# Seven-product pairs in a two-layer decoder trunk: partial sums seeded into the PSUM banks instead of added behind them

## What is computed

```python
for layer in range(2):                 # D = 2048, 256 tokens, fp32
    if layer == 0: h = h + fox_mixer(rmsnorm(h, g), ...)        # 16 heads of attention
    else:          h = h + retention_mixer(rmsnorm(h, g), ...)  # 8 heads, q/k 256, v/gate 512 wide
    h = h + square(relu(rmsnorm(h, g) @ w_up)) @ w_down         # D_FF = 8192
return rmsnorm(h, final_norm)
```

## Time and profile before

| | us |
|---|---|
| median of three executions | 2486.71 |
| span of the profiled execution, first to last instruction | 2485.3 |
| TensorE busy | 2474.5 |
| VectorE busy | 1915.0 |
| ScalarE busy | 1402.3 |
| mean granted TensorE clock | 0.999 |

### The profile page before, as it was taken

One profiled execution on the slowest core, in us unless ns is written; L12 is line 12 of the kernel. 1 busy time (PEld: TensorE's weight loads), 2 busy tenths in 40 slices (PEclk: granted clock), 3 DMA queues, 4 the chain that ended last, 5 costly groups with the idle time before them and its releaser, 6 DMA issues.

```text
span 2485.3 us, 30031 instructions
## 1 busy us (share of the span) xinstructions
PE 2474.5 (100%) x11128; PEld 2050.7 (83%) x11128; DVE 1915.0 (77%) x2118; ACT 1402.3 (56%) x1689; POOL 158.6 (6%) x272
## 2 busy tenths in 40 slices
PE   9999999999999999999999999999999999999998
PEld 7888888888888888888888888888888888888887
DVE  6455555887978888987778868778988888788787
ACT  7454445554646555655556545656565555464564
POOL 0000000100100000101110001000010000010010
PEclk9999999999999999999999999999999999999999
DMA  8445456675756766766665665666677666666584
GB/s 312 158 155 182 140 200 218 214 253 182 260 202 222 248 208 229 237 212 204 219 225 184 231 201 183 199 206 233 236 248 245 207 231 229 211 237 237 192 273 146
DMA packets 148503, 534.83 MB, mean 215 GB/s; under 512 B 18704, under 2 KB 18960, under 8 KB 147472
## 3 DMA queue, kind: packets, MB, share of 16 engines
q1 hardware_dynamic: 131040, 476.65, 55.1%
q0 software_dynamic: 17184, 56.11, 7.9%
q10 hardware_dynamic: 144, 0.26, 0.0%
HBM read 506.74 MB, written 26.21 MB: 214 GB/s over the span
## 4 chain that ended last, share of the span: by engine, by line
PE 53%; DVE 2%; issue 1%; DMA 1%; ACT 1%; POOL 0%; DVEq 0%; ACTq 0%; POOLq 0%
PE acc L905 9%; PE acc L907 9%; PE acc L906 9%; PE sc L907 7%; PE sc L906 7%; PE sc L905 7%; PE mix L906 1%; PE mix L907 1%; PE mix L905 1%; DVE w_lo L1916 1%; ACT w_hi L1339 0%; DMA raw<-in_w_stream 0%; DMA evac<-park 0%; PE tr L1054 0%; PE tr L703 0%
## 5 line engine op out<-in xcount | busy, mean ns | idle before, releaser
L1916 DVE TENSOR_TENSOR w_lo<-raw,w_hi 128x1024 fp32r<-128x1024 f32 x696 | 847.1, 1230 | 290.4 <-ACT w_hi L1339 287.8
L1339 ACT ACTIVATE w_hi<-raw 128x1024 fp32r<-128x1024 f32 x696 | 727.8, 1058 | 571.8 <-PE sc L907 185.3
L905 PE MATMUL acc<-w_hi,xT_hi 128*128 128x512 f32 x826 | 322.6, 391 | 1.0 <-DVE xT_lo L1981 0.6
L907 PE MATMUL acc<-w_hi,xT_lo 128*128 128x512 f32 x826 | 321.6, 389 | 0.0
L906 PE MATMUL acc<-w_lo,xT_hi 128*128 128x512 f32 x826 | 321.5, 389 | 0.0
L1339 ACT ACTIVATE w_hi<-scratch 128x1024 fp32r<-128x1024 f32 x201 | 211.8, 1057 | 169.3 <-PE acc L907 74.4
L1916 DVE TENSOR_TENSOR w_lo<-scratch,w_hi 128x1024 fp32r<-128x1024 f32 x201 | 244.7, 1220 | 68.1 <-ACT w_hi L1339 67.5
L905 PE MATMUL sc<-w_hi,xT_hi 128*128 128x512 f32 x736 | 287.4, 390 | 0.0
L907 PE MATMUL sc<-w_hi,xT_lo 128*128 128x512 f32 x736 | 286.6, 389 | 0.0
L906 PE MATMUL sc<-w_lo,xT_hi 128*128 128x512 f32 x736 | 286.4, 389 | 0.0
L905 PE MATMUL acc<-w_hi,aT_hi 128*128 128x512 f32 x600 | 233.8, 390 | 0.0
(11 more groups left out here) (279 smaller groups left out, 3930.5 us busy)
## 6 DMA issues: line engine op xcount, KB each, us to landing
raw<-in_w_stream SPq DMA_DIRECT2D x725, 512.0 KB, 4.6
scratch<-in_w_stream SPq DMA_DIRECT2D x171, 512.0 KB, 4.8
park<-stage POOLq DMA_DIRECT2D x38, 512.0 KB, 3.2
evac<-park POOLq DMA_DIRECT2D x152, 128.0 KB, 3.2
gain<-in_gains POOLq DMA_DIRECT2D x4, 1024.0 KB, 8.1
qk_park<-evac POOLq DMA_DIRECT2D x8, 512.0 KB, 4.8
scratch<-qk_park POOLq DMA_DIRECT2D x32, 128.0 KB, 5.3
h<-in_x SPq DMA_DIRECT2D x2, 1024.0 KB, 8.7
```

The lines of the kernel that those rows point to most:

```text
L905: pe.matmul(bank[:, :], x_hi, w_hi[:, c], start=start, stop=False, skip_group_check=True)
L907: return pe.matmul(bank[:, :], x_lo, w_hi[:, c], start=False, stop=stop, skip_group_check=True)
L1339: act.activation(w_hi[:, slot * SW:(slot + 1) * SW], mlp_raw(u, load_of(u, t)), ACT.Copy).then_inc(mlp_hi, 1)
L1916: dve.tensor_tensor(w_lo[:, c], mlp_raw(u, load_of(u, t)), w_hi[:, c].bitcast(F32), ALU.subtract).then_inc(mlp_lo, 1)
```

## The change

Three partial sums are written into PSUM banks ahead of the products that use them, and these products accumulate onto them. With P1 in bank x after B11 and P5 in `mix[1]` after TAU1:

- `seed_u` (ScalarE): x is copied to `mix[0]`; TAU2 accumulates there and gives U.
- `copy_p5` (ScalarE): `mix[1]` is copied to SBUF.
- `seed_z` (ScalarE): U is copied from `mix[0]` to z; TAU3 accumulates there and gives V in z.
- `seed_e` (VectorE): e = P5 - U; B22 accumulates.
- `seed_w` (VectorE): w = P5 - z, which must be read between TAU3 and TAU4; the products of block 1, token tile 1 accumulate.

The lead-in's order becomes B11, TAU1, TAU2, B21, TAU3, B22, TAU4. Each output is complete in its bank: `copy_t1`, `copy_p7`, `u_part`, `v_part`, `g_part`, `fold` and `sum_to` are gone. Signs of S2 and S4 change in the sums. VectorE's `tau13` is split: `tau3` comes after `lo(B21)`. In `value_gate_pair` both seeds of VectorE come after `lo(TAU4)` and both `rotated` after the seeds; in `seven_pair` `seed_w` comes before `lo(7)` and the second `turn_blocks` after it. Gates of six heads are read by `silu` from the bank; heads 3 and 7 get a copy (`gate_copy`).

```diff
-B11, TAU1, TAU3, B21, TAU2, B22, TAU4 = range(SEVEN)
+B11, TAU1, TAU2, B21, TAU3, B22, TAU4 = range(SEVEN)
...
@@ gpsimd, head
-                    pool.wait_ge(silu_made[t], hd + 1)
+                    if ends_half(hd):
+                        pool.wait_ge(silu_made[t], hd // RET_HALF + 1)
+                    else:
+                        pool.wait_ge((e_out, w_out)[t], UNITS[head_unit(hd) + 1].pairs + 1)
...
@@ tensor, seven_pair
                 pe.wait_ge(s_lo, unit.sums)
-                wait(pe, v_made, unit.sevens)
+                wait(pe, p5_out, unit.sevens)
                 wait(pe, o_out, TOKS * heads_done)
                 block_sum(u, TAU1, mix[1], lambda kk: s_part(up, S1, kk), True, True)
-                pe.wait_ge(w_out if after_block else z_out, unit.pairs)
-                block_sum(u, TAU3, z, lambda kk: s_part(up, S3, kk), True, True)
-                pe.wait_ge(t1_out, unit.sevens + 1)
+                pe.wait_ge(u_seeded, unit.sevens + 1)
+                block_sum(u, TAU2, mix[0], lambda kk: s_part(up, S2, kk), False, True)
                 block_sum(u, B21, x, lambda kk: x_part(lhs, 0, 2 + kk), False, False)
                 between(B21)
-                wait(pe, u_made, unit.sevens)
-                block_sum(u, TAU2, mix[0], lambda kk: s_part(up, S2, kk), True, True)
...
-                block_sum(u, B22, e, lambda kk: s_part(up, S4, kk), True, False)
+                pe.wait_ge(z_seeded, unit.sevens + 1)
+                block_sum(u, TAU3, z, lambda kk: s_part(up, S3, kk), False, True)
+                between(TAU3)
+                pe.wait_ge(e_seeded, unit.sevens + 1)
+                block_sum(u, B22, e, lambda kk: s_part(up, S4, kk), False, False)
                 between(B22)
-                pe.wait_ge(p7_out, unit.sevens + 1)
+                pe.wait_ge(w_seeded, unit.sevens + 1)
                 block_sum(u, TAU4, z, lambda kk: x_part(lhs, 1, 2 + kk), False, False)
...
@@ scalar
+            def seed_u(u, heads_done=0):
+                wait_used(act, u, B11)
+                wait(act, e_seeded, UNITS[u].sevens)
+                wait(act, o_out, TOKS * heads_done)
+                act.activation(mix[0][:, :], banks_of(u)[0][:, :], ACT.Copy).then_inc(u_seeded, 1)
+            def copy_p5(u, parts=mlp_parts):
+                wait_used(act, u, TAU1)
+                wait(act, w_seeded, UNITS[u].sevens)
+                act.activation(parts[1], mix[1][:, :], ACT.Copy).then_inc(p5_out, 1)
+            def seed_z(u, after_block=False):
+                wait_used(act, u, TAU2)
+                act.wait_ge(w_out if after_block else z_out, UNITS[u].pairs)
+                act.activation(banks_of(u)[1][:, :], mix[0][:, :], ACT.Copy).then_inc(z_seeded, 1)
...
@@ scalar, value_gate_pair
-                hi(u, TAU2)
+                hi(u, TAU3)
                 hi(u, B22)
+                seed_u(u, hd)
                 for t in range(TOKS):
                     act.wait_ge(qk_done[t], hd + 1)
                     act.activation(evac[t][:, :], banks_of(u - 1)[t][:, :], ACT.Copy,
                                    scale=factor(t, rstd)).then_inc(qk_out[t], 1)
-                copy_t1(u, sums_made, ret_parts)
                 hi(u, TAU4)
-                copy_p7(u, ret_parts)
+                copy_p5(u, ret_parts)
+                seed_z(u, after_block=True)
...
@@ vector
+            def seed_e(u, parts=mlp_parts, after_block=False):
+                dve.wait_ge(p5_out, unit.sevens + 1)
+                dve.wait_ge(z_seeded, unit.sevens + 1)
...
+                dve.tensor_tensor(banks_of(u)[2][:, :], parts[1], mix[0][:, :], ALU.subtract).then_inc(e_seeded, 1)
+            def seed_w(u, parts=mlp_parts, after_block=False):
+                wait_used(dve, u, TAU3)
...
+                dve.tensor_tensor(w[:, :], parts[1], z[:, :], ALU.subtract).then_inc(w_seeded, 1)
...
@@ vector, seven_pair
+                lo(u, TAU4)
+                seed_e(u)
...
-                lo(u, TAU4)
+                seed_w(u)
                 if was_normed and not end:
                     gained_after(1, p_quad + 1, w_out, done, stage if by_pe else tr)
+                lo(u, 7)
                 if turn is not None and not by_pe:
                     turn_blocks(turn + 1)
-                lo(u, 7)
...
@@ vector, value_gate_pair
-                tau13(u)
+                tau1(u)
                 lo(u, TAU1)
                 tau2(u)
...
-                lo(u, TAU3)
+                lo(u, TAU2)
...
                 lo(u, B21)
+                tau3(u)
                 if hd == 0:
                     norm_for_mixer()
-                lo(u, TAU2)
+                lo(u, TAU3)
                 tau4(u)
                 lo(u, B22)
+                lo(u, TAU4)
+                seed_e(u, ret_parts, after_block=True)
+                seed_w(u, ret_parts, after_block=True)
                 rotated(hd, 0)
-                lo(u, TAU4)
                 dve.wait_ge(rotated_made, TOKS * hd + 1)
                 rotated(hd, 1)
                 lo(u, 7)
                 turn_qk_blocks(hd)
```

More of the change, by code:

```diff
@@ L522, in wait_sum @@
         def wait_sum(eng, u, tau):
-            eng.wait_ge(sum_made, 4 * UNITS[u].sevens + (TAU1, TAU3, TAU2, TAU4).index(tau) + 1)
+            eng.wait_ge(sum_made, 4 * UNITS[u].sevens + (TAU1, TAU2, TAU3, TAU4).index(tau) + 1)
         @block.sync
@@ L998, in seven_pair @@
                     half, s = rest_of(u, r)
[L999 to L1006, removed]
+                    if end and half == 1:
+                        one_token_at_a_time(u)
+                        return
                     if half == 0 and turned and s == REST - 2:
@@ L1032, in between @@
                 def between(t):
-                    if was_normed and t == TAU2:
+                    if was_normed and t == TAU3:
                         own()
@@ L1334, in hi @@
                     act.wait_ge(w_used, T("block") * (SLOTS - 1) + (slot + 1))
-                if UNITS[u].kind == SEVEN_PAIR and t in (TAU1, TAU3, TAU2, TAU4):
+                if UNITS[u].kind == SEVEN_PAIR and t in (TAU1, TAU2, TAU3, TAU4):
                     wait_sum(act, u, t)
@@ L1344, in s_high, with copy_full, relu @@
                 act.activation(w_hi[:, s_cols(up)], sums, ACT.Copy).then_inc(s_hi, 1)
-            def copy_full(u, parts=mlp_parts):
-                wait(act, u_made, UNITS[u].sevens)
+            def copy_full(parts):
                 act.activation(parts[0], tr[1][:, :], ACT.Copy).then_inc(full_out, 1)
-            def copy_t1(u, sums_made, parts=mlp_parts):
+            def seed_u(u, heads_done=0):
                 wait_used(act, u, B11)
[L1354 to L1363, removed]
+                wait(act, e_seeded, UNITS[u].sevens)
[9 more added lines that the diff above has]
+                act.activation(banks_of(u)[1][:, :], mix[0][:, :], ACT.Copy).then_inc(z_seeded, 1)
+            def relu(tok, done, bank, out, count, n=0):
                 act.wait_ge(done, count)
@@ L1451, in seven_pair @@
                 dst = xT_hi if was == "normed" else aT_hi
-                was_plain, was_up, was_normed, was_head = (was == k for k in ("plain up", "up", "normed", "head"))
+                was_up, was_normed, was_head = (was == k for k in ("up", "normed", "head"))
                 by_pe = was_normed and now == "up"
-                if was_up:
-                    squared_relu_of_sum(1, z_out, done)
                 late_norm = was_normed and u - 1 in LATE
@@ L1463, in seven_pair @@
                 hi(u, TAU1)
-                hi(u, TAU3)
+                hi(u, TAU2)
                 if was_head:
@@ L1535, in mlp_pair_of @@
                 u = mlp_unit(m, i)
-                was = ("plain up" if m == 0 and i == 1 else "normed" if i in (0, PAIRS - 1)
-                       else "up" if (i - 1) % 4 < 2 else "down")
+                was = "normed" if i in (0, PAIRS - 1) else "up" if (i - 1) % 4 < 2 else "down"
                 new_sums = (0, X_SUMS_OF_MLP - 1)[m] + 1 + (i - 1) // 4 + 1 if (i - 1) % 4 == 0 else 0
@@ L1673, in _ @@
         def _(dve):
-            T = Tally("block", "hi0", "hi1", "step", "norm", "mixer_norm", "group", "ret_head", "full", "folded")
+            T = Tally("block", "hi0", "hi1", "step", "norm", "mixer_norm", "group", "ret_head", "full")
             def step(ins):
@@ new lines, in seed_w, with tau1 @@
+            def seed_w(u, parts=mlp_parts, after_block=False):
+                unit = UNITS[u]
+                wait_used(dve, u, TAU3)
+                if after_block:
+                    dve.wait_ge(qk_out[1], unit.ones)
+                else:
+                    dve.wait_ge(w_out, unit.pairs)
+                z, w = banks_of(u)[1], banks_of(u)[3]
+                dve.tensor_tensor(w[:, :], parts[1], z[:, :], ALU.subtract).then_inc(w_seeded, 1)
+            def tau1(u):
+                r11, r12 = (mlp_raw(u, load) for load in (0, 1))
@@ L2175, in seven_pair @@
                     turn_lo(turn + 1, *dst, p_quad + 1)
```

(5 more changed lines are left out.)

214 lines of the change are left out of this document (81 added, 133 removed).

## The result

The changed kernel takes 2556.1 us (median of four executions, 2551.7 to 2558.8), the kernel before 2486.6 beside it: ratio 1.0275, 95% interval 1.0263 to 1.0288, or 69.5 us more. The prediction said 2524, range 2508 to 2546. Direction right, size too small, outside the range. The profiled execution took 2558.8 with a span of 2557.0, so the span is 71.7 longer than before.

What follows compares the result with a forecast made beforehand. TensorE's unbroken row of matmuls was taken as the bound, with only 0.9 us of waits inside. Heads 33.8 plus other pairs 3.1 gave 36.9; added to 2486.7 that is 2523.6, so 2524 us, range 2508 to 2546.

Steps and rivals of the forecast that it cites:

- what can't be won: Whole kernel: at most 0.9 us of TensorE's inside waits can go; some 110 us less VectorE work gains nothing.
- the place and the size of the stall: Eight value and gate pairs, before tile 7: rotations behind `seed_w` wait for TAU3, so TensorE loses 3.7 us in each.
- bank-to-bank copies: Seeds, an unseen operation: priced from near rows at 0.60 us on ScalarE and 0.69 on VectorE.
- rival of late channel mixers: 31 channel-mixer pairs: a step or release taking 0.4 us more loses some 0.5 each, 16 in all, 2540; chance 0.14.
- the tail's first stretch: After the last matmul, 2478.2 to 2482.0: TensorE idle 3.8 us at full clock, used as evidence against a falling clock.
- the rival of a falling clock: Behind each head's stall: one tile at 1.2 instead of 2.4 GHz, 2.7 us more each, 22 in all, 2546; chance 0.07.
- Other pairs ... together 3.1: First pair of second mixer about 1.7 us, last pair of first mixer 0.9, four `wo` pairs 0.5: 3.1 lost.
- in heads 1 and 5 alone: Expected sign: TensorE waits on ScalarE's `seed_u` only in these heads, where TAU2 loses 1.6 us.
- the heads without it: Eight value and gate pairs, no clock loss: five at 3.7 us, head 0 at 4.1, heads 1 and 5 at 5.6: 33.8.
- behind two more `hi` at 3.3: First pair of the second mixer: VectorE is behind, `seed_u` goes out at 3.3 us, the chain ends about 1.7 late.
- the common pairs: 29 of 31 channel-mixer pairs: every seed and low part in time by 0.4 to 0.8 us, cost 0.
- The four `wo` pairs: These pairs lose 0.5 us together, in one `lo(7)` behind two SiLUs, in another behind two gain products.

Runs made afterwards that it cites:

- C: The changed kernel itself, with the seeds and the new order as the change describes, against the kernel before: 2556.1 us, ratio 1.0275.
- the last two runs: Changed kernel with `tau3` early and rotations parted, plus either the `wo` order changed (2503.4 us) or the transposition ahead of `lo(8)` (2503.6 us).

## Why the prediction was off

**Right: what can't be won.** Fewer semaphore waits and folds, 93 us less of VectorE, gave nothing back, and the matmuls kept their distance of 0.23 wherever nothing was late. The amounts were off (110 less forecast on VectorE; 26 more on ScalarE, 9 measured), but both were priced at nothing, and rightly.

**Right: the place and the size of the stall.** Forecast 3.7 us in each value and gate pair, measured 3.98 - 0.227 = 3.8 in each, with every step from `seed_w` on within 0.1 us of the forecast. Ahead of it one reading was off and cost nothing: VectorE stood still for 0.87 before `seed_w`, not for about 2.5, because it had waited 1.19 and 0.26 for ScalarE before and began `seed_e` only at 5.44; the wait for TAU3 ended last all the same. In head 1 gives the first matmul one matmul too early: the pair begins at 1176.14, so the wait for `seed_u` comes to 1.4 by the same working, and 1.3 was measured. The cause was the one named: the rotations stand behind a wait for TensorE's own position. It is shown from both sides, by the kernel before with the rotations held (stalls of 3.0 and 2.1) and by C with them parted (none).

**Right: bank-to-bank copies.** ScalarE's were taken at 0.60 and VectorE's at 0.69. The groups of C:

```profile
L2028 DVE TENSOR_TENSOR sc<-scratch,acc 128x512 f32<-128x512 f32 x35 | 24.3, 694 | 29.8 <-PE acc L911 29.8
...
L1349 ACT ACTIVATE mix<-acc 128x512 f32<-128x512 f32 x39 | 22.1, 566 | 2.3 <-PE acc L911 2.1
```

0.57 and 0.69. The rival of late channel mixers, slow copies in each of 31 pairs, did not come: 22 of them lose nothing. Its amount of 16 us was nearly there for another reason, told below: the other nine lose 13.6. With `tau3` in its old place 29 pairs lose nothing and two lose 0.2 and 1.1.

**Wrong: the clock.** "Against it: the tail's first stretch is 3.8 us of idle engine at the full clock." That row gave the rival of a falling clock its 0.07. The fallen clock cost 17 to 19 us, four fifths of the 22 that the rival named and half of what was missing. The step that failed is reading one row as a rule: it shows that TensorE *can* idle 3.8 us at 1.00, once. Here all eight stalls of 3.6 brought the clock down, six of eight at 3.0, five of eight at 2.1 (each in one profiled execution). The Trainium skill, "TensorE: Matmul & The Clock Gate", section "Why this matters for your kernels", says that idle gaps between bursts throw the engine back to half speed; the traces agree, with 0.50 behind C's stall. With the rival's 22 the sum would have been 2546, still 10 short.

**Wrong: "Other pairs ... together 3.1", and waits on `seed_u` "in heads 1 and 5 alone".** The first term measured 15.1 without the clock (16.3 less 1.2), with 1.2 more in the last pair, and the heads without it 38.0 instead of 33.8. `seed_u` was late in head 0 too, in the last pair of the first mixer and in four pairs of the second. In the first pair of the second mixer (first matmul 1864.14) I let it go out "behind two more `hi` at 3.3"; it went out at 4.2. Timeline of ACT, `hi(TAU3)` and `seed_u`:

```profile
1866.47 1.06 ACT L1334 ACTIVATE w_hi<-scratch 128x1024 fp32r<-128x1024 f32 x1 [2.67 <-DVE scratch L2042]
...
1868.38 0.58 ACT L1349 ACTIVATE mix<-acc 128x512 f32<-128x512 f32 x1
```

ScalarE stands still for `tau3`, and `seed_u` stands behind that tile and the next in its list. For the common pairs I had `lo(TAU4)` done at 5.0 and `seed_e` at 5.7; in pair 7 of the first mixer they were done at 6.7 and 7.3. I counted each `hi` and each sum by its duration; I did not count that VectorE stands still for 1.19 in the round trip of each of the first three sums there, nor that the pairs that follow a late pair (3, 7, 11 and the last) have two residual adds between them. `tau3`'s move I described and costed only where the norm or `s_sums` stood behind it. The run with `tau3` early takes out 12.8 us, and with it all of `seed_u`'s waits. The four `wo` pairs measured 3.8 instead of 0.5, most of it two waits of 1.05 before tile 7, which `tau3`'s place does not touch.

**What the 69.5 are made of**, by what each kernel takes more than the kernel before beside it (C 69.5, `tau3` early 56.3, with matmuls in the gap 37.0, with the rotations parted 15.9): 13.2 the place of `tau3`; 19.3 the clock; 21.1 the rotations behind the seeds; 15.9 remain. The eight stalls alone are worth 30, so the parted order must lose 9 of them again elsewhere. The shares hold for this order of steps: put into C itself, the same matmuls gave back only 10.4, and why is open. What remains is mostly waits around the heads (12.4 in the heads and 2.9 in the `wo` pairs by the timeline), moved but not lessened by the last two runs. Whether a further order would remove them wasn't tried, and no version was found that beats the kernel before: with its row of matmuls unbroken there was nothing for the seeds to win.

## What to carry to other kernels

When TensorE has no gap, saving work on other engines is worth nothing, and the question for each new wait is what stands behind it in its engine's list and when that is due. A sum that VectorE makes, ScalarE rounds and VectorE splits needs its whole round trip (here 3.6 us) in the plan, and needs other work to lie inside it. Stalls of 2 to 4 us in a kernel that TensorE bounds are to be priced with a fallen clock behind them, here 2.3 us more for each of eight stalls of 3.6, and matmuls into a free bank in the gap kept it up.

## What was new about the hardware

- The clock at one and the same gap of 2.09 us fell in five cases of eight and held in three, with 1.00 and 0.57 granted behind the gap in neighbouring heads. What decides between them stays open.
- C's clock also fell behind the 2.0 us wait in the first pair of the second mixer, and behind none of its shorter ones; with the rotations parted, two waits of 1.8 and 1.9 left it up, and with the changed `wo` order one of 2.15 did not. With the low parts between the rotations, six waits of 2.2 to 3.4 brought it down, and two of 2.96 and 2.86 before the scores of heads 1 and 3 left it at 1.00.
- The fall can come after the gap: in heads 1, 4 and 5 of C the first matmuls of tile 7 still stood 0.23 to 0.35 apart, and the granted clock fell 0.6, 1.5 and 0.8 us after tile 7 had begun.
- After a fall the distance of 0.43 us held for 5 to 8 matmuls or for 11 to 13, and then was 0.23 again at once. That is so behind all 28 falls of C, of the run with `tau3` early, and of the runs with the stall of 3.0 and with the stall of 2.1.
